# Gate tiles of a hybrid MLA and retention layer in pairs by seven block products, values of retention formed inside attention

## The chip, the cores and the metric

The kernel runs on one core of one Trainium2 chip. The metric is the device time of one execution in microseconds (us). PE is TensorE, DVE is VectorE, ACT is ScalarE, POOL is GpSimd, and SP is the engine whose queue starts nearly all transfers.

## What is computed

One decoder layer over 1024 tokens of 1024 channels, with two branches that run beside each other: MLA (8 heads) and chunkwise retention (4 heads of 256 query and key channels and 512 value channels, 8 chunks of 128 tokens). Both branches are gated and merged by sigmoid gates:

```python
mod = jax.nn.silu(c) @ w_ada[l] + b_ada[l]
shift, scale, gate = jnp.split(mod[:, None, :], 3, axis=-1)
h = rmsnorm(x, g_pre[l]) * (1.0 + scale) + shift
proj = h @ w_in[l]
(c_q, c_kv, k_pe, gate_mla, q_ret, k_ret, v_ret, gate_ret,
 merge_mla, merge_ret) = jnp.split(proj, pts, axis=-1)
y_mla = mla_branch(c_q, c_kv, k_pe, positions, g_q[l], w_q_up[l], g_kv[l], w_kv_up[l])
y_mla = y_mla * jax.nn.silu(gate_mla)
y_ret = retention_branch(q_ret, k_ret, v_ret, positions, g_ret[l]) * jax.nn.silu(gate_ret)
merged = (jax.nn.sigmoid(merge_mla) * (y_mla @ w_proj_mla[l])
          + jax.nn.sigmoid(merge_ret) * (y_ret @ w_proj_ret[l]))
x = x + gate * (merged @ w_out[l])
return rmsnorm(x, g_final)
```

The first product, `h @ w_in`, has 9,920 output columns. 5,120 of them are gates: `gate_mla` (1,024), `gate_ret` (2,048), `merge_mla` and `merge_ret` (1,024 each). `v_ret` has 2,048.

## The kernel before

**Products.** Every float32 product is made of three matmuls. Each operand is split in a high part (a copy rounded to the type that TensorE multiplies) and a low part (the operand minus its high part); high by high, low by high and high by low are summed in PSUM. A weight tile is 128 output columns by 1024 input channels, 512 KB. SP loads it into `w_raw` (`load_weight`, L428), ACT writes `w_hi` (`split_weight`, L437), DVE writes `w_lo` (`lower_weight`, L445). These three buffers have three slots (RING). A tile of `h @ w_in` is 48 matmuls of 128x512 (2 halves of the tokens, 8 blocks of input channels, 3 products) into two PSUM banks.

**Order of the weight tiles.** A list written out by hand, SEQ, gives the order in which SP, ACT, DVE and PE go through the weight tiles: first `l` (6 tiles: latents of q, of k and v, and k_pe), then `m` (8 MLA gate tiles), then one by one tiles of the up-projections (`q`, `a` and `b` with the rotary part of q, `k`, `v`; 18 to 36 or so short matmuls) and the 16 tiles `g` of retention's gate, then the 16 tiles `x` of retention's q and k, which are called turned here, with the four `v` tiles between the first of them. Gate tiles are activated by ACT and stored to DRAM (`act_t`).

**Turned tiles.** Two `x` tiles make one pair of rotated tiles: DVE multiplies each by cosine and sine (`rot_products`, L1164), POOL adds and subtracts (L837, L839), ACT and DVE split (L981, L1141) into three slots of `split_stage`, and SP stores the parts to DRAM (`store_turned`, L597; L592 stores `rot` as well for a k pair). SP does this in iteration r of one loop, which goes: load the weight tile r+4, do the loads of `w_ada_gate` for the gate row (L530, at tiles behind the last `v`), then store tile r. A load waits until the slot's old tile was lowered; SP holds everything behind an instruction that waits.

**Values of retention.** `r`: 16 weight parts, each two blocks of input channels by 512 columns, four parts for each head. Their 768 matmuls stand in a stretch of their own behind the turned tiles, one PSUM bank for each of 8 token tiles (V_BANKS), evicted in four slots of `v_stage`.

**Attention** goes in 64 steps (8 heads, 8 blocks of queries). Between its parts PE does other products as filler (`fill`, L1696), so many a step (FILL_STEP): the 16 merge gate tiles `f`, 768 matmuls. **Retention** then goes in 32 steps, and behind it the merge of both branches and the output product.

## Time and profile before

| | |
|---|---|
| three runs | 1700.97, 1701.58, 1703.8 us (median 1701.58) |
| the profiled execution | 1702.75 us, its span 1700.8 us |
| PE busy | 1653.4 us, 97% of the span |
| DVE, ACT, POOL busy | 807.4, 526.5, 76.9 us (47%, 31%, 5%) |
| DMA | 308.04 MB, 181 GB/s in the mean |

Stages by the clock of the profile, in us from the span's start: norm and modulation to about 74; `l` tiles to 109; `m` tiles to 199; up-projections and gates to 504; `v` and turned tiles to 643; values of retention to 825; attention to about 1188; then retention, merge and output. A row of the profile's timeline gives the start, the duration, the engine, the line, the operation and its tiles; in brackets stands how long the engine was idle before, and what released it.

### The profile page before, as it was taken

How to read it: one execution, taken by the hardware profiler on the slowest of the kernel's cores; microseconds unless marked ns; L12 is line 12 of the kernel's file. 1: busy time of each engine (PE TensorE's matmuls, PEld its weight loads, DVE VectorE, ACT ScalarE, POOL GpSimd, SP SyncE). 2: the span in 40 equal slices, each digit the busy share in tenths (PEclk: the TensorE clock that was granted, in tenths of full speed). 3: DMA queues.
4: the chain of work that ended last, by engine and by line, in shares of the span. 5: the costliest groups of instructions: out<-in, count | busy, mean ns of one | idle time of the engine just before them, and what ended most of it. 6: DMA issues, size and time to landing. Idle time of an engine off the chain costs nothing.

```text
span 1700.8 us, 20129 instructions
## 1 busy us (share of the span) xinstructions
PE 1653.4 (97%) x8020; PEld 1383.2 (81%) x8020; DVE 807.4 (47%) x1259; ACT 526.5 (31%) x887; POOL 76.9 (5%) x37
## 2 busy tenths in 40 slices
PE   4999999999999999999999999999899999999998
PEld 3787888888888888788788888888688887888886
DVE  6913523132345764222445555545466666545443
ACT  5443322222123211222333343434343344212211
POOL 2200001010111221000000000000000000000000
PEclk8999999999999999999999999999899999999999
DMA  9032344435377669543344444446988886523322
GB/s 388 17 109 81 107 151 149 150 130 210 130 253 256 209 209 298 209 149 146 151 158 163 154 159 163 167 140 218 382 258 275 268 268 219 209 99 136 130 89 85
DMA packets 167435, 308.04 MB, mean 181 GB/s; under 512 B 11312, under 2 KB 104368, under 8 KB 162224
## 3 DMA queue, kind: packets, MB, share of 16 engines
q1 hardware_dynamic: 167056, 306.70, 52.5%
q8 instruction: 64, 1.05, 0.2%
q14 instruction: 27, 0.22, 0.0%
q10 hardware_dynamic: 288, 0.07, 0.0%
HBM read 195.57 MB, written 110.62 MB: 180 GB/s over the span
## 4 chain that ended last, share of the span: by engine, by line
PE 88%; DVE 4%; DMA 3%; issue 2%; ACT 1%; SPq 1%; POOL 1%; ACTq 0%; DVEq 0%; POOLq 0%
PE p_banks L1696 10%; PE p_banks L1588 10%; PE p_banks L1587 10%; PE p_banks L1586 10%; PE p_banks L1726 5%; PE p_banks L1896 3%; PE p_banks L1898 3%; PE p_banks L1897 3%; PE p_banks L1645 3%; PE p_banks L1646 3%; PE p_banks L1647 3%; PE p_banks L1795 2%; PE p_banks L1946 2%; PE p_banks L1944 2%; PE p_banks L1945 2%
## 5 line engine op out<-in xcount | busy, mean ns | idle before, releaser
L445 DVE TENSOR_TENSOR w_lo<-w_raw,w_hi 128x1024 fp32r<-128x1024 f32 (+3 forms) x126 | 149.9, 1190 | 314.1 <-ACT w_hi L437 314.0
L1586 PE MATMUL p_banks<-h_hi,w_hi 128*128 128x512 f32 x688 | 269.2, 391 | 1.6 <-DVE w_lo L445 1.6
L1587 PE MATMUL p_banks<-h_lo,w_hi 128*128 128x512 f32 x688 | 267.7, 389 | 0.0
L1588 PE MATMUL p_banks<-h_hi,w_lo 128*128 128x512 f32 x688 | 267.7, 389 | 0.0
L437 ACT ACTIVATE w_hi<-w_raw 128x1024 fp32r<-128x1024 f32 x125 | 118.8, 952 | 325.7 <-PE p_banks L1647 102.2
L1586 PEld LDWEIGHTS p_banks<-h_hi,w_hi 128*128 128x128 f32 x688 | 129.2, 188 | 29.4 <-DVE w_lo L445 2.0
L1587 PEld LDWEIGHTS p_banks<-h_lo,w_hi 128*128 128x128 f32 x688 | 129.2, 188 | 27.4 <-issue 0.7
L1588 PEld LDWEIGHTS p_banks<-h_hi,w_lo 128*128 128x128 f32 x688 | 129.2, 188 | 26.7
L1696 PE MATMUL p_banks<-h_hi,w_hi 128*128 128x512 f32 x256 | 105.6, 413 | 1.8 <-DVE v_stage L1306 1.8
L1696 PE MATMUL p_banks<-h_lo,w_hi 128*128 128x512 f32 x256 | 105.3, 411 | 0.0
L1696 PE MATMUL p_banks<-h_hi,w_lo 128*128 128x512 f32 x256 | 105.1, 411 | 0.0
L1645 PE MATMUL p_banks<-w_hi,h_hi 128*128 128x512 f32 x256 | 100.9, 394 | 2.5 <-DVE v_stage L1306 2.3
L1646 PE MATMUL p_banks<-w_hi,h_lo 128*128 128x512 f32 x256 | 100.3, 392 | 0.0
L1647 PE MATMUL p_banks<-w_lo,h_hi 128*128 128x512 f32 x256 | 100.2, 391 | 0.0
L1896 PE MATMUL p_banks<-y_hi,w_hi 128*128 128x512 f32 x256 | 99.6, 389 | 0.0
L1897 PE MATMUL p_banks<-y_lo,w_hi 128*128 128x512 f32 x256 | 99.6, 389 | 0.0
L1898 PE MATMUL p_banks<-y_hi,w_lo 128*128 128x512 f32 x256 | 99.6, 389 | 0.0
L1001 ACT ACTIVATE prob<-p_banks,neg_max 128x128 f32<-128x128 f32 (+3 forms) x64 | 47.5, 742 | 143.1 <-DVE neg_max L1323 143.1
L1323 DVE TENSOR_REDUCE neg_max<-p_banks 128x1 f32<-128x128 f32 (+3 forms) x64 | 48.5, 758 | 80.1 <-PE p_banks L1758 80.1
L962 ACT ACTIVATE stage<-p_banks 128x512 f32<-128x512 f32 x48 | 26.1, 595 | 177.6 <-PE p_banks L1588 177.6
L1362 DVE TENSOR_TENSOR pt_lo<-p_banks,pt_hi 128x512 fp32r<-128x512 f32 (+2 forms) x96 | 51.8, 554 | 47.5 <-ACT pt_hi L1018 47.4
L1018 ACT ACTIVATE pt_hi<-p_banks 128x512 fp32r<-128x512 f32 (+2 forms) x96 | 46.0, 490 | 61.2 <-PE p_banks L1795 60.4
(221 smaller groups left out, 3250.2 us busy)
## 6 DMA issues: line engine op xcount, KB each, us to landing
w_raw<-in_w_dense SPq DMA_DIRECT2D x102, 512.0 KB, 5.7
act_t<-stage SPq DMA_DIRECT2D x80, 256.0 KB, 2.1
qk_chunk<-qk_chunks SPq DMA_DIRECT2D x32, 640.0 KB, 5.1
qk_chunks<-split_stage SPq DMA_DIRECT2D x32, 512.0 KB, 5.8
v_ret<-v_stage SPq DMA_DIRECT2D x32, 512.0 KB, 3.6
v_chunk<-v_ret SPq DMA_DIRECT2D x32, 512.0 KB, 5.8
merge_t<-act_t SPq DMA_DIRECT2D x48, 256.0 KB, 3.2
ada<-in_w_ada SPq DMA_DIRECT2D x4, 2048.0 KB, 23.8
```

The costliest lines, as they stand in the source:

```text
L437: self.nc.scalar.activation(self.w_hi[:, r % RING, 0:width], self.w_raw[:, r % RING, 0:width], ACT.Copy)\
L445: self.nc.vector.tensor_tensor(self.w_lo[:, r % RING, 0:width], self.w_raw[:, r % RING, 0:width], self.w_hi[:, r % RING, 0:width].bitcast( ...
L1586: nc.tensor.matmul(out, w_hi[:, slot, cut], x_hi[:, k, tok], start=(k == ks[0]), stop=False)
L1587: nc.tensor.matmul(out, w_hi[:, slot, cut], x_lo[:, k, tok], start=False, stop=False)
L1588: ins = nc.tensor.matmul(out, w_lo[:, slot, cut], x_hi[:, k, tok], start=False, stop=(k == ks[-1]))
L1645: nc.tensor.matmul(out, h_hi[:, k, tok], w_hi[:, slot, cut], start=(k == 0), stop=False)
L1646: nc.tensor.matmul(out, h_lo[:, k, tok], w_hi[:, slot, cut], start=False, stop=False)
L1647: last = nc.tensor.matmul(out, h_hi[:, k, tok], w_lo[:, slot, cut], start=False, stop=(k == KD - 1))
L1696: ins = nc.tensor.matmul(out, w[:, slot, k * P:(k + 1) * P], x[:, k, tok], start=(m == 0), stop=(m == UNIT - 1))
L1896: self.nc.tensor.matmul(out, self.w_hi[:, slot, cut], self.y_hi[y][:, tok], start=(k == 0), stop=False)
L1897: self.nc.tensor.matmul(out, self.w_hi[:, slot, cut], self.y_lo[y][:, tok], start=False, stop=False)
L1898: return self.nc.tensor.matmul(out, self.w_lo[:, slot, cut], self.y_hi[y][:, tok], start=False, stop=(k == KD - 1))
```

## The change

**Gates in pairs.** The 40 gate tiles (8 `m`, 16 `g`, 16 `f`) become 20 pairs of tiles. A pair is a product of two blocks of columns, by two halves of the input channels, by two halves of the tokens: eight block products of 12 matmuls. The change makes it by seven (`pair_products`; the seven forms of Strassen's kind): 84 matmuls of 128x512 in place of 96. For this h gets four sums over its blocks (`h_sum`, 128x2048 each, each split in two parts), and each pair four sums of weight blocks of 128x512 on POOL; ACT writes a high part for each of the seven forms (`high_form`), one copy of a product and four activations; DVE writes seven low parts and five sums of outputs (`pair_outputs`), all 128x512. A pair's weights come as one load of 1 MB (`w_pairs`). Five slots hold the forms.

**Order.** k_pe's tile comes first, then the five other latents, then all 20 pairs, then `x0` to `x5`, and then the up-projections with little between them. The norms of the latents (squares, row sums, roots, reciprocals, `c_hi`, `c_lo`) now stand beside `x0` to `x2`. SP loads tile r+3 in iteration r, where it loaded r+4. The tables of rotation and k_rope go through DRAM.

**Values of retention inside attention.** Their 768 matmuls are now the filler: FILL_START is 36 products ahead of the first scores, then FILL_STEP. The weight parts all go through slot 0 of `w_raw`, and each load waits until the part before was lowered. `v_stage` has two slots; `lower_fill` makes the low part on DVE.

The diff, cut to its core:

```diff
-SEQ = [("l", n) for n in range(LAT_TILES)] + [("m", n) for n in range(H_MLA)]
-for n in range(GATES):
-    SEQ += [UPS[n], ("g", n)]
-for n in range(TURNS):
-    SEQ += UPS[GATES + n:GATES + n + 1] + [("x", n)]
-R_UP = LAT_TILES + H_MLA
+SEQ = [("l", K_PE)] + [("l", n) for n in range(K_PE)]
+R_UP = len(SEQ)
+SEQ += [("x", n) for n in range(6)]
+SEQ += [("q", 0), ("q", 1), ("q", 2), ("q", 3), ("a", 0), ("b", 0), ("x", 6), ("q", 4), ("q", 5), ("x", 7),
+        ("q", 6), ("q", 7), ("a", 1), ("b", 1), ("x", 8), ("k", 0), ("k", 1), ("k", 2), ("k", 3), ("x", 9)]
+for n in range(4):
+    SEQ += [("k", 4 + n), ("v", n)]
+SEQ += [("x", n) for n in range(10, TURNS)]
...
+FILL_START = 36
+FILL_STEP = [12, 12, 12, 11, 11, 10, 9, 9]
...
+    def raw_place(self, r):
+
+        return self.w_raw[:, 0 if R_V <= r < R_MERGE else r % RING, 0:self.weight(r)[1]]
...
+        if R_V <= r <= R_MERGE + 1:
+            sp.wait_ge(self.w_lo_ready, r if r <= R_MERGE else R_MERGE)
...
+            self.load_weight(sp, r + RING)
...
+        self.load_weight(sp, R_V + RING)
+        sp.wait_ge(self.rot_made, self.rot_total)
+        self.load_v(sp, 0)
+        sp.wait_ge(self.gate_step, KD + 2)
...
+            nc.gpsimd.tensor_tensor(total, a21, a22, ALU.add).then_inc(self.form_sums, 1)
+            nc.gpsimd.tensor_tensor(a21, a11, a21, ALU.subtract).then_inc(self.form_sums, 1)
...
+            pe.wait_ge(self.form_lo, SUMS + f + 1)
...
+            for q in range(KD // 2):
+                cut = slice(q * P, (q + 1) * P)
+                self.nc.tensor.matmul(out, w_hi[:, cut], x_hi[:, q, :], start=fresh and q == 0, stop=False,
+                                      skip_group_check=True)
+                self.nc.tensor.matmul(out, w_hi[:, cut], x_lo[:, q, :], start=False, stop=False, skip_group_check=True)
+                last = self.nc.tensor.matmul(out, w_lo[:, cut], x_hi[:, q, :], start=False, stop=q == KD // 2 - 1,
+                                             skip_group_check=True)
...
+        self.fill(pe, FILL_START)
...
+            if tile == 0 and not first and kind == 0:
                 pe.wait_ge(self.w_lo_ready, r + 1)
```

SP's queue at the end of the turned tiles, before: L428 loads a weight, L530 a block of `w_ada_gate`, L592 and L597 store a k pair, L597 alone a q pair; the last rows are k pair `x15`, the gate row, and the first loads for attention.

```order
L428 DMA w_raw<-in_w_dense 128x1024 [waits w_lo_ready] x2
L592 DMA qk_chunks<-rot 128x8x128 [waits rot_added]
L597 DMA qk_chunks<-split_stage 128x8x128 [waits split_lo_ready]
L597 DMA qk_chunks<-split_stage 128x8x128
L592 DMA qk_chunks<-rot 128x8x128 [waits rot_added]
L597 DMA qk_chunks<-split_stage 128x8x128 [waits split_lo_ready]
L597 DMA qk_chunks<-split_stage 128x8x128
L428 DMA w_raw<-in_w_dense 128x1024 [waits w_lo_ready]
L552 DMA gate_rows<-gate_row 128x1024 [waits gate_step]
L428 DMA w_raw<-in_w_dense 128x1024 [waits w_lo_ready] x2
L604 DMA q_even<-q_hl 128x2048 [waits split_stored_2,split_stored_1,rot_stored,split_stored_0,gate_row_stored]
```

The same place after the change, from behind the stores of `x11` on; here L469 loads a weight, L640 a block of `w_ada_gate`, L702 stores. The first L469 loads `x15`, the next four the first four value parts.

```order
L469 DMA w_raw<-in_w_dense 128x1024 [waits w_lo_ready]
L640 DMA ada_gate_w<-in_w_ada_gate 128x1024 [waits gate_step] x2
L469 DMA w_raw<-in_w_dense 128x1024 [waits w_lo_ready]
L640 DMA ada_gate_w<-in_w_ada_gate 128x1024 [waits gate_step] x2
L702 DMA qk_chunks<-split_stage 128x8x128 [waits split_lo_ready]
L702 DMA qk_chunks<-split_stage 128x8x128
L702 DMA qk_chunks<-split_stage 128x8x128 [waits split_lo_ready]
L702 DMA qk_chunks<-split_stage 128x8x128
L469 DMA w_raw<-in_w_dense 128x1024 [waits w_lo_ready]
L646 DMA k_rope<-k_rope 128x2048 [waits split_stored_2,ret_tables_stored,split_stored_1,split_stored_0]
```

Behind these rows come the loads for the first head, the load of the third part, the six stores of `x15`, and the load of the fourth part. The loads of the value parts moved in between gate row blocks and stores, and four of them are wanted at once.

PE at the start of attention after the change: L1845 is the row sum for the gate row, L1927 the filler, L1985 the first scores; each wait for `w_lo_ready` is for one value part.

```order
L1845 MATMUL p_banks<-gate_row,ones 128x512 [waits split_lo_ready,gate_step]
L1845 MATMUL p_banks<-gate_row,ones 128x512
L1927 MATMUL p_banks<-w_hi_aside,h_hi 128x512 [waits rot_products,w_lo_ready]
...
L1927 MATMUL p_banks<-w_hi,h_hi 128x512 [waits w_lo_ready]
...
L1927 MATMUL p_banks<-w_hi,h_hi 128x512 [waits w_lo_ready]
...
L1927 MATMUL p_banks<-w_hi,h_hi 128x512 [waits w_lo_ready]
...
L1985 MATMUL p_banks<-k_even,q_even 128x128 [waits late_consts_loaded,consts_split,ret_tables_loaded,gate_step,qk_even_loaded]
```

Six filler products stand between one wait for a part and the next, and the row sum now stands at the very end of the turned tiles, where it stood three tiles behind the last gate block.

## Rows read from the trace of the kernel before

**Rows 1.** The page: busy time and share of the span, by engine.

```profile
PE 1653.4 (97%) x8020; PEld 1383.2 (81%) x8020; DVE 807.4 (47%) x1259; ACT 526.5 (31%) x887; POOL 76.9 (5%) x37
```

**Rows 2.** Windows: stretch, its length, busy time of PE, PEld, DVE, ACT, POOL, PE clock, DMA.

```profile
109.00:199.00 90.00, 90.00 (x391) 73.15 (x390) 42.00 (x27) 35.68 (x42) 0.00 (x0) 1.00 0.24 81
504.00:643.00 139.00, 137.93 (x670) 115.97 (x669) 88.41 (x70) 32.88 (x39) 28.22 (x10) 1.00 0.71 232
643.00:825.00 182.00, 179.53 (x782) 146.49 (x781) 46.93 (x50) 38.51 (x47) 4.76 (x2) 0.99 0.53 186
825.00:1188.00 363.00, 361.02 (x2081) 313.83 (x2081) 185.75 (x378) 143.82 (x310) 0.00 (x0) 1.00 0.48 167
```

**Rows 3.** Timeline of PE: two matmuls, 66 apart in a gapless stretch.

```profile
184.30 0.39 PE L1586 MATMUL p_banks<-h_hi,w_hi 128*128 128x512 f32 x1
...
199.26 0.39 PE L1586 MATMUL p_banks<-c_hi,w_hi 128*128 128x512 f32 x1
```

**Rows 4.** Waits of PE over the span: total, times, longest.

```profile
PE p_banks L1811 <- DMA qk_chunk<-qk_chunks: 7.2, 2, 6.4
...
PE p_banks L1645 <- DVE v_stage L1306: 2.3, 4, 1.6
```

**Rows 5.** Timeline of PE at the start of attention.

```profile
827.24 0.47 PE L1696 MATMUL p_banks<-h_hi,w_hi 128*128 128x512 f32 x1 [1.81 <-DVE v_stage L1306]
...
829.20 0.63 PE L1696 MATMUL p_banks<-h_hi,w_lo 128*128 128x512 f32 x1
829.63 0.63 PE L1696 MATMUL p_banks<-h_hi,w_hi 128*128 128x512 f32 x1
```

**Rows 6.** Timeline behind a second turned tile (k pair): DVE.

```profile
556.34 2.35 DVE L1164 TENSOR_TENSOR rot<-p_banks,ret_tables_back 128x1024 f32<-128x1024 f32 x2 [1.69 <-PE p_banks L1588]
558.61 2.51 DVE L445 TENSOR_TENSOR w_lo<-w_raw,w_hi 128x1024 fp32r<-128x1024 f32 x1
561.16 4.58 DVE L1141 TENSOR_TENSOR split_stage<-rot,split_stage 128x1024 fp32r<-128x1024 f32 x2
...
574.09 1.22 DVE L445 TENSOR_TENSOR w_lo<-w_raw,w_hi 128x1024 fp32r<-128x1024 f32 x1
```

**Rows 7.** The same pair: POOL, SP's queue; then a q pair: DVE, SP.

```profile
557.64 2.39 POOL L837 TENSOR_TENSOR rot<-rot 128x1024 f32<-128x1024 f32 x1 [28.62 <-DVE rot L1164]
...
570.57 1.70 SPq L428 DMA_DIRECT2D w_raw<-in_w_dense  x1
...
522.49 1.23 DVE L1164 TENSOR_TENSOR rot<-p_banks,ret_tables_back 128x1024 f32<-128x1024 f32 x1 [2.21 <-PE p_banks L1588]
...
534.10 1.81 SPq L428 DMA_DIRECT2D w_raw<-in_w_dense  x1
```

**Rows 8.** A k pair beside the gate row's blocks: DVE, SP's queue, DVE, ACT.

```profile
599.85 2.36 DVE L1164 TENSOR_TENSOR rot<-p_banks,ret_tables_back 128x1024 f32<-128x1024 f32 x2 [3.77 <-PE p_banks L1588]
...
622.11 2.57 SPq L428 DMA_DIRECT2D w_raw<-in_w_dense  x2
...
626.74 2.67 DVE L1296 SCALAR_TENSOR_TENSOR gate_row<-ada_gate_w,silu_c,gate_row 128x1024 f32<-128x1024 f32 x2
...
629.61 1.06 ACT L437 ACTIVATE w_hi<-w_raw 128x1024 fp32r<-128x1024 f32 x1 [17.75 <-DMA w_raw<-in_w_dense]
```

**Rows 9.** DMA issues, KB and us to landing: windows 130:430 (two), 601:645.

```profile
w_raw<-in_w_dense SPq DMA_DIRECT2D x20, 512.0 KB, 5.7
w_raw<-in_w_q_up SPq DMA_DIRECT2D x12, 192.0 KB, 3.0
...
w_raw<-in_w_dense SPq DMA_DIRECT2D x4, 512.0 KB, 7.3
```

**Rows 10.** Groups of DVE's instructions, window 100:504: busy, mean ns, idle before.

```profile
L1273 DVE RECIPROCAL latent_total<-latent_total 128x1024 f32<-128x1024 f32 x2 | 13.1, 6554 | 3.4 <-ACT latent_total L918 3.4
...
L1280 DVE TENSOR_TENSOR latent<-latent,latent_total 128x1024 f32<-128x1024 f32 x5 | 5.8, 1219 | 0.0
```

**Rows 11.** Timeline of ACT at the first `v` tile.

```profile
506.53 0.60 ACT L981 ACTIVATE split_stage<-p_banks 128x512 fp32r<-128x512 f32 x1 [5.28 <-DMA qk_chunks<-split_stage]
```

More of the change, by code:

```diff
@@ L34 @@
 ACT_TILES = 40
-MASKED = -1e30
+MASKED = -2.0 ** 100
 TURN_1 = 6.28125
@@ L374, in counts @@
             elif kind in "abx":
+                self.rot_pair[r], self.k_turns[r] = rot // 4, turned
+                turned += kind == "x" and i % 4 == 3
                 rot += 2
@@ L521, in sync @@
                 sp.dma_start(self.ret_tables[:, :, :], d["ret_tables"].rearrange("a p n -> p a n"))\
                     .then_inc(self.tables_loaded, 16)
+            for n, out in enumerate((1, 0, 2, 3)):
+                tile, half = ((0, 0), (1, 1), (1, 0), (0, 1))[out]
+                sp.wait_ge(self.evicted, self.latent_evicted + 5 * pair + 2 + n)
+                sp.dma_start(d["act_t"][2 * pair + tile][:, half * HALF:(half + 1) * HALF], self.out_stage[out])\
+                    .then_inc(self.stored[out], 16)
@@ L523, in sync @@
+        for r in range(R_UP, R_V):
+            kind, i = SEQ[r]
+            self.load_weight(sp, r + RING)
             if r == R_GATE_ROW:
@@ L713, in sync_retention @@
                 self.load_t(sp, 1)
-            if n == 4:
-                for half in range(2):
-                    sp.wait_ge(self.stored[half], 16 * (H_MLA + GATES + FILL_TILES))
             if n + 3 < CHUNK_STEPS:
@@ L1241, in vector @@
+        self.lower_weight(dve, R_UP + 2)
+        for n, (b, i, squares) in enumerate(((0, 1, 3), (0, 2, 4), (1, 4, 5))):
+            dve.wait_ge(self.squared, NT + squares)
+            if n == 1:
+                dve.wait_ge(self.lat_added, 1)
+            nc.vector.tensor_tensor(self.total[:, b, :], self.total[:, b, :], self.places[i], ALU.add)\
+                .then_inc(self.lat_added, 1)
+        for r in range(R_UP, R_V):
+            kind, i = SEQ[r]
             if kind in "qk":
@@ L1655, in tensor, with pair_products @@
         self.tensor_output(pe)
+    def pair_products(self, pe, pair):
+        h = [self.h_hi, self.h_lo]
+        even, odd = (slice(e, KD, 2) for e in range(2))
+        low, high = slice(0, HALF), slice(HALF, S)
+        sums = [(self.h_sum_hi[n], self.h_sum_lo[n]) for n in range(SUMS)]
+        operands = [[x[:, even, low] for x in h], sums[0], sums[1], sums[2], [x[:, odd, low] for x in h], sums[3],
+                    [x[:, odd, high] for x in h]]
+        for n in range(FORMS):
+            f = FORMS * pair + n
+            out = self.p[:, self.form_bank(pair, (0, 1, 2, 3, 0, 4, 1)[n]), :]
+            fresh = n not in (4, 6)
+            pe.wait_ge(self.form_lo, SUMS + f + 1)
+            if n == 0:
+                if pair < 2:
+                    pe.wait_ge(self.evicted, self.latent_evicted - 2)
+                else:
+                    pe.wait_ge(self.pair_done, SUMS + 5 * (pair - 1))
+            elif pair == 0 and n in (1, 2):
+                pe.wait_ge(self.evicted, self.latent_evicted - 2 + n)
+            elif pair and n == 3:
+                pe.wait_ge(self.evicted, self.latent_evicted + 5 * pair - 2)
+            elif n == 4:
+                pe.wait_ge(self.evicted, self.latent_evicted + 5 * pair + 1)
+            elif pair and n == 5:
+                pe.wait_ge(self.pair_done, SUMS + 5 * pair)
+            elif n == 6:
+                pe.wait_ge(self.pair_done, SUMS + 5 * pair + 3)
+            w_hi, w_lo = (self.form[f % FORM_SLOTS][:, low_part, :] for low_part in range(2))
+            x_hi, x_lo = operands[n]
+            for q in range(KD // 2):
[5 more added lines that the diff above has]
+                                             skip_group_check=True)
+            last.then_inc(self.form_summed, 1)
     def v_up(self, pe, r):
```

828 lines of the change are left out of this document (479 added, 349 removed).

## The prediction

> **What bounds the kernel now.** I read the page first: PE is busy 97% of the span, DVE 47%, ACT 31%, POOL 5% [rows 1], so PE's stream sets the time, and an engine beside it matters where it keeps PE waiting. Then the windows, to see where PE is idle: 0 in the 90 us of gates, 1.1 us in the turned tiles (139.00 − 137.93), 2.5 in the values of retention, 2.0 in attention [rows 2]. Then the pace: two matmuls 66 apart start 14.96 us apart, so one of 128x512 costs 0.2267 us, whatever the 0.39 of its record [rows 3]. At that pace the 768 matmuls of the values are 174.1 us, and their stretch ran from 643.3 to 824.7: some 7.2 us more than its work. The waits of PE name v_stage for 2.3 of them, and the chunks of retention for 7.2 us elsewhere [rows 4]. Attention starts with a wait of 1.81 us [rows 5].
>
> The clock shows there too: behind that wait matmuls start 0.43 us apart in place of 0.23 (829.20, 829.63) [rows 5], which is the lower of the two levels (1.2 and 2.4 GHz), for about 10 matmuls, 2 us. So the start of attention costs 3.8 us.
>
> **What is removed.** 40 gate tiles of 48 matmuls become 20 pairs of 84: 1,920 − 1,680 = 240 matmuls, 240 × 0.2267 = **54.4 us** [rows 3]. The stretch of the values goes: its 768 matmuls take the place of the 768 of the merge gates in attention, at the same price, and its 7.2 us of stalls with it; so do the 3.8 at the start of attention and the 1.1 of the turned tiles. Gains: 54.4 + 7.2 + 3.8 + 1.1 = **66.5 us**.
>
> **What is added beside PE.** A pair gives PE 84 × 0.2267 = 19.0 us. DVE gets 12 instructions of 128x512 in it; one of 128x1024 takes 1.22 us [rows 10], half of it 0.61, with a fixed part some 0.69: 8.3 us. ACT gets 12 of about 0.6: 7.1. POOL gets 4 sums; one of 128x1024 takes 2.39 [rows 7], half of it 1.2: 4.8. All lie under 19.0, and the forms are made up to four ahead, so I cost them at nothing. If POOL and DVE slow each other, the trace has a price: the w_lo of 558.61 took 2.51 us, POOL working from 557.64 on, and that of 574.09 took 1.22 [rows 6, 7]. All seven low parts at double price would make DVE 13 us a pair, still under 19.0.
>
> The Trainium skill speaks against this placing of sums: its page "SBUF — State Buffer", under "SBUF: two separate sides", says that a DVE instruction with both inputs in SBUF and a GpSimd one that reads SBUF exclude each other for the whole instruction. By that rule the two engines' times add up, 8.3 + 4.8 = 13 us, and the pair stays bound by PE; the trace agrees with the rule (2.51 beside 1.22).
>
> The four sums of h and their splits go on DVE ahead of the first pair, beside the latents' tiles; an estimate from instructions of 1.22 us for 1,024 columns has the first low part ready at 109 us, when PE ends the latents; bounds 0 and 3 us, I take 1.
>
> **What moves, projections.** Before, each short up-projection tile had a full tile of 10.9 us behind it. Now they stand in a row, and SP loads tile r+3 right behind the stores of tile r−1. Behind a k pair's second tile that load goes out 14.2 us after PE ends (556.34 to 570.57), behind a q pair's 11.6 (522.49 to 534.10) [rows 6, 7]. It lands in 3.0 us for a q tile, 5.7 for a full one, 7.3 under stores [rows 9], and then come w_hi and w_lo (1.1 us for a short tile, 2.3 to 3.6 for a full one [rows 6, 8]). So the fourth tile behind a turned pair can't start before +17 to +19 us, and the three in between cover it for 48 × 0.2267 = 10.9 each if full, but 18 × 0.2267 = 4.1 if `q`, 2.7 if `k`.
>
> - DVE first: x0 to x2 (32.6 us of PE) carry the two reciprocals 13.1, five products 5.8, c_lo about 6.2, squares' sums 3.7 [rows 10], beside two or three rotations 2.35, low parts 1.2 to 2.5 and splits 4.6 [rows 6]: 46 in all, begun at 10.9, the end of x0. So DVE is at 57 then, at 62 with x3's rotation and a w_lo; x3's splits are out at 70 and q1's weight is lowered at 76.3, where PE is there at 6 × 10.9 + 4.1 = 69.4: q1 waits 6.9.
> - x5, then q0, q1, q2 (12.3 us): q3 waits 7.3, with DVE's lateness in it.
> - x7, then q6, q7, a1: 14.2 + 0.5 + 3.0 + 1.1 = 18.8, less 12.3: 6.5; I take 6.3 (4.8 to 7.8).
> - k0 to k2 (8.2) cover the load of x9 (5.7 and 2.3, and the store ahead): 3.9.
> - x9, then k4, v0, k5 (11.1): v1 waits 5.9. The splits of v0 to v3 wait for stores to leave the three slots, as before, where one such wait was 5.28 us and full tiles hid it [rows 11]: 1.8 for v1, 4.2 for v2, 4.3 for v3. Small ones 0.9.
>
> Sum 6.9 + 7.3 + 6.3 + 3.9 + 7.7 + 4.2 + 4.3 + 0.9 = 41.5, call it **42 us**. Nothing excludes that waits merge, since a stall gives SP time for the next: low end 15; high end 50.
>
> **What moves, into attention.** I count from the end of x11, where PE has 43.6 us of x12 to x15 left. SP issues the stores of x11 and then the load of x15 at +22.3 (599.85 to 622.11) [rows 8]; it lands at 29.8 (7.3 [rows 9]) and is lowered at 32. Blocks 2 and 3 of the gate row are added at 34.6 (2.67 for two [rows 8]). The first value part is loaded at 35.7, lowered at 43.7. Then x13's splits, 46; blocks 4 and 5, 48.6; its four stores and the loads of blocks 6 and 7 to 53; the second part lands at 60.5, is lowered at 62.7; blocks 6 and 7 are added at 65.3. Only then can the row sum run, for which PE has waited since 43.6: 21.7 us. The third part is lowered at about 72. The fourth waits in SP behind the six stores of x15: issued at 78, lowered at 87.9. PE wants it after the row sum and 18 products, nominally at 49.4. So PE loses 87.9 − 49.4 = **38 us** up to the first scores; what lies behind DVE and SP there (scores, softmax) has nothing else to run on. Low end 8 if the loads are not held by the gate row, high end 45.
>
> In attention the parts come one by one through one slot; 16 − 4 loads over 64 steps of 5.7 us (363 / 64 [rows 2]) leave the time, but at the three changes of head the lowering must fit behind the last use: 0 to 6, I take **2**. At the start of retention three more loads of 512 KB join the chunks, which PE already waits 7.2 us for [rows 4]: 0 to 5, I take **2**. The clock falls after each long wait; at 2 us each [rows 5] and some eight waits, half of them where PE waits anyway: 5 to 16, I take **7**.
>
> The Trainium skill, page "TensorE: Matmul & The Clock Gate", under "HAM oscillation — how this bites in real kernels", says that waits for DMA throttle PE again and again, and cost beyond the wait itself. The trace agrees (0.43 for 0.23 us), and this is a point against the change that a count of matmuls misses.
>
> **Sum**, against the profiled execution's 1702.75 (span 1700.8, 1.2 above the median of the runs): 1702.75 − 66.5 + 42 + 38 + 2 + 2 + 1 + 7 = 1728.3; less 1.2: **1727 us** as a median.
>
> **The rivals.**
> (B) It gets faster: one mechanism, that PE's waits in the projections let SP run ahead, so the loads around the gate row go out early and the transition costs the 8 us of its low end, while the projections keep 30. 1702.75 − 66.5 + 30 + 8 + 12 − 1.2 = 1685. For it: SP's lateness is counted from PE's ends, and each stall gives it time. Against: at 622.11 the load was late though no tile before it was [rows 8]. It turns faster when both terms together fall under 54 us.
> (C) Weight tiles hide everywhere, as before the waits of PE in these stages were few [rows 2]: 1701.6 − 66.5 + 7 = 1642.
> (D) The seven products are bound by POOL or DVE after all, if a sum of 128x512 on POOL costs 3 us and more, as a fixed part would make it: 2 us a pair, 40 on top: 1767.
> (E) No change, gains and waits equal: 1698 to 1705.
>
> **How the numbers follow.** A measurement of this kernel tells about 0.2%, 3.4 us, from no change. My forecast (own range 1712 to 1745) has 0.67, B 0.13, C 0.07, D 0.08, E 0.05. Slower is forecast and D, 0.75; same 0.05; faster B and C, 0.20. The range leaves C and D out (0.15) and a little at B's edge: 1679 to 1750.
>
> **What would show it.** In the profile after: 240 matmuls fewer on PE; the pairs with PE gapless for 380 us (20 × 19.0); waits of PE for w_lo before q1, q3, b1, x9, v1; and for the gate row and w_lo at L1845 and L1927, some 38 us in a place. SP's queue should show the fourth value part's load behind the stores of x15. I am wrong if PE is not idle at L1845 and L1927, or if the forms wait for POOL.

## The result and the profile after

The changed kernel takes 1791.06 us in the median of four runs (1788.92 to 1795.02), the kernel before 1701.28: a ratio of 1.0527 with a 95% interval of 1.0506 to 1.0548. It is slower by 90 us, where 25 were forecast, and outside the range of 1679 to 1750. The page of the profile after, busy time by engine and the clock granted to PE in 40 slices of the span:

```profile
PE 1625.2 (91%) x7780; PEld 1353.8 (76%) x7780; DVE 940.2 (53%) x1467; ACT 579.9 (32%) x1005; POOL 188.0 (11%) x117
...
PEclk8999999999998989997899999989899999999999
```

PE has the 240 matmuls less (7,780 for 8,020 [rows 1]), and is busy 28.2 us less in a span that is 86.2 us longer (1787.0 for 1700.8). So its idle time grew from 47.4 to 161.8 us, by 114.4. 240 matmuls are 54.4 us; busy time fell by 26.2 less than that. Most of these 26.2 are matmuls at the lower clock: by the clock's records PE is busy for 67.1 us at the lower level, where it was 21.4, and half of the difference is 22.8; the other 3.4 are not assigned. Below, "the clock" stands for the whole 26.2. 114.4 + 26.2 − 54.4 = 86.2: that is the whole result, and it falls into stages. Windows (length, busy time of PE, PEld, DVE, ACT, POOL, clock, DMA):

```profile
109.00:490.00 381.00, 380.34 (x1677) 314.65 (x1678) 174.69 (x242) 141.79 (x242) 108.15 (x78) 1.00 0.30 111
490.00:760.00 270.00, 228.81 (x1033) 188.38 (x1032) 148.04 (x124) 73.74 (x93) 35.89 (x14) 0.92 0.55 188
760.00:870.00 110.00, 72.07 (x290) 56.92 (x289) 45.76 (x37) 16.16 (x16) 15.15 (x6) 0.83 0.69 222
870.00:1252.00 382.00, 353.88 (x1985) 305.25 (x1984) 192.97 (x390) 135.13 (x296) 0.00 (x0) 0.96 0.46 161
1262.00:1310.00 48.00, 28.45 (x141) 23.33 (x140) 20.98 (x53) 14.88 (x29) 0.00 (x0) 0.79 0.93 342
```

The first is the pairs: PE gapless at full clock, 20 pairs in 381 us. The seven products do what they are for. The others are the projections, the last turned tiles with the start of attention, attention, and the start of retention. PE's waits give the same places by what ended them (us in total, times, longest):

```profile
PE p_banks L1796 <- DVE w_lo L495: 31.5, 6, 8.2
PE p_banks L1845 <- DVE gate_row L1472: 20.2, 1, 20.2
PE p_banks L1958 <- DVE w_lo L495: 19.6, 1, 19.6
PE p_banks L1985 <- ACT prob L1156: 18.2, 3, 6.7
PE p_banks L1927 <- DVE w_lo L495: 17.7, 2, 14.7
...
PE p_banks L2007 <- DMA v_head<-v_hl: 9.9, 3, 3.5
PE p_banks L1903 <- DVE w_lo L495: 8.0, 2, 7.4
...
PE p_banks L1903 <- DVE split_stage L1304: 3.3, 3, 1.5
...
PE p_banks L1885 <- DVE w_form L1423: 1.1, 1, 1.1
```

L1796 and L1903 are the projections: 31.5 + 8.0 + 3.3 = 42.8 us. L1845 and L1927 are the gate row and the value parts at the start of attention: 37.9. L1985 and L2007 are attention: 28.1. L1985 makes the scores, which wait until ACT has made the exp of the step before (`prob`); L2007 makes the products with v. L1958 is the merge product that fills retention: 19.6, where the wait of 7.2 for chunks is gone [rows 4].

How these waits come about is read from the queues. In the projections, the longest one (8.18 us, before q1) reads like this, with DVE, SP and ACT (SPq is SP's queue):

```profile
550.57 2.35 DVE L1324 TENSOR_TENSOR rot<-p_banks,ret_tables_back 128x1024 f32<-128x1024 f32 x2
...
560.52 3.32 SPq L702 DMA_DIRECT2D qk_chunks<-split_stage  x2
563.88 3.10 SPq L469 DMA_DIRECT2D w_raw<-in_w_q_up  x2
...
570.92 1.00 ACT L489 ACTIVATE w_hi<-w_raw 128x384 fp32r<-128x384 f32 x2 [12.87 <-DMA w_raw<-in_w_q_up]
```

SP issues q1's weight right behind the last stores of x2 and x3, and ACT stands 12.87 us until it lands. The stores are late because DVE came to the rotation of x3 only at 550.57, 12.7 us after PE had ended x3 (537.9), behind the low parts of the latents. So both causes of the prediction are in this one wait: DVE is late, and the place of the load behind the stores hands that on.

In attention, SP and ACT and PE around 950 us:

```profile
949.88 0.32 SPq L771 DMA_DIRECT2D v_ret<-v_stage  x1
950.24 0.43 SPq L469 DMA_DIRECT2D w_raw<-in_w_dense  x1
...
954.43 1.06 ACT L489 ACTIVATE w_hi<-w_raw 128x1024 fp32r<-128x1024 f32 x1 [8.46 <-DMA w_raw<-in_w_dense]
955.40 0.99 ACT L1156 ACTIVATE prob<-p_banks,neg_max 128x896 f32<-128x896 f32 x1
...
956.53 0.80 PE L1985 MATMUL p_banks<-k_odd,q_odd 128*128 128x512 f32 x1 [5.99 <-ACT prob L1156]
```

The value part's load is issued behind a value store, for whose low part SP waits; ACT stands 8.46 us for the load, and the exp of the step stands behind it on ACT. PE's wait is put down to the exp, which is ready in a microsecond. The load of v_head has the same neighbour:

```profile
923.34 0.32 SPq L771 DMA_DIRECT2D v_ret<-v_stage  x1
923.70 0.58 SPq L719 DMA_DIRECT2D v_head<-v_hl  x1
```

At the start of retention, the chain of what ended last:

```profile
1273.93 2.82 SPq L798
1276.86 4.69 SPq L851
...
1283.23 10.11 DMA v_ret<-v_stage
...
1294.01 1.05 ACT w_hi L489
```

and ACT's timeline there:

```profile
1293.43 0.69 ACT L1183 ACTIVATE v_stage<-p_banks,ret_cols 128x512 fp32r<-128x512 f32 x1 [20.11 <-DMA v_ret<-v_stage]
```

ACT stands 20.1 us before the eviction of the last value unit, since the unit before it has the same stage slot and its store was issued late and took 10 us; the high part of the merge weight that PE wants stands behind it.

And nearly every long wait leaves the clock low, as in [rows 5]. PE waits 15 times over 2 us behind the pairs; after 13 of these waits the clock's records have the lower level for another 3 to 6 us. Here behind the one of 8.18 us:

```profile
572.09 0.79 PE L1796 MATMUL p_banks<-c_hi,w_hi 128*128 128x512 f32 x1 [8.18 <-DVE w_lo L495]
...
573.53 0.63 PE L1796 MATMUL p_banks<-c_hi,w_hi 128*128 128x512 f32 x1
573.96 0.63 PE L1797 MATMUL p_banks<-c_lo,w_hi 128*128 128x512 f32 x1
```

### The profile page after: what moved, and what is told of

Read it like the earlier page. It is cut to its first block, busy times and chain, and to the rows that moved or that the text cites. A ratio compares the mean times of both kernels' runs of the same rounds, so it can differ in the third digit from the quotient of the medians.

```text
span 1787.0 us, 20246 instructions
## 1 busy us (share of the span) xinstructions
PE 1625.2 (91%) x7780; PEld 1353.8 (76%) x7780; DVE 940.2 (53%) x1467; ACT 579.9 (32%) x1005; POOL 188.0 (11%) x117
## 4 chain that ended last, share of the span: by engine, by line
PE 71%; DVE 9%; DMA 9%; SPq 3%; POOL 2%; issue 2%; ACT 2%; ACTq 0%; DVEq 0%; POOLq 0%
PE p_banks L1927 9%; PE p_banks L1885 7%; PE p_banks L1887 7%; PE p_banks L1888 7%; DMA w_raw<-in_w_dense 5%; PE p_banks L1958 5%; PE p_banks L2132 3%; PE p_banks L2131 3%; PE p_banks L2130 3%; PE p_banks L2029 2%; SPq L702 2%; PE p_banks L2180 2%; PE p_banks L2179 2%; PE p_banks L2178 2%; DVE split_stage L1304 1%
## 5 line engine op out<-in xcount | busy, mean ns | idle before, releaser
L489 ACT ACTIVATE w_hi<-w_raw 128x1024 fp32r<-128x1024 f32 (+3 forms) x81 | 72.3, 894 | 371.0 <-DMA w_raw<-in_w_dense 157.6
L495 DVE TENSOR_TENSOR w_lo<-w_raw,w_hi 128x1024 fp32r<-128x1024 f32 (+2 forms) x82 | 94.8, 1157 | 143.1 <-ACT w_hi L489 143.0
L1423 DVE TENSOR_TENSOR w_form<-w_pair,w_form 128x512 fp32r<-128x512 f32 x120 | 92.9, 775 | 102.0 <-ACT w_form L1090 100.8
L1090 ACT ACTIVATE w_form<-w_pair 128x512 fp32r<-128x512 f32 x120 | 75.6, 632 | 195.1 <-PE p_banks L1888 187.1
L1796 PE MATMUL p_banks<-h_hi,w_hi 128*128 128x512 f32 x304 | 120.8, 397 | 7.6 <-DVE w_lo L495 7.6
L1797 PE MATMUL p_banks<-h_lo,w_hi 128*128 128x512 f32 x304 | 119.4, 393 | 0.0
L1798 PE MATMUL p_banks<-h_hi,w_lo 128*128 128x512 f32 x304 | 119.3, 392 | 0.0
L1927 PE MATMUL p_banks<-w_hi,h_hi 128*128 128x512 f32 x192 | 80.7, 420 | 17.7 <-DVE w_lo L495 17.7
L1885 PE MATMUL p_banks<-h_hi,w_form 128*128 128x512 f32 x240 | 93.5, 389 | 1.1 <-DVE w_form L1423 1.1
L1888 PE MATMUL p_banks<-h_hi,w_form 128*128 128x512 f32 x240 | 93.4, 389 | 0.0
L1887 PE MATMUL p_banks<-h_lo,w_form 128*128 128x512 f32 x240 | 93.4, 389 | 0.0
L1927 PE MATMUL p_banks<-w_lo,h_hi 128*128 128x512 f32 x192 | 80.6, 420 | 0.0
L1927 PE MATMUL p_banks<-w_hi,h_lo 128*128 128x512 f32 x192 | 80.2, 418 | 0.0
L1796 PEld LDWEIGHTS p_banks<-h_hi,w_hi 128*128 128x128 f32 x304 | 57.7, 190 | 21.3 <-DVE w_lo L495 8.9
L1958 PE MATMUL p_banks<-y_hi,w_hi 128*128 128x512 f32 x128 | 52.1, 407 | 19.6 <-DVE w_lo L495 19.6
```

The source lines that it names most:

```text
L495: self.nc.vector.tensor_tensor(self.lo_place(r), self.raw_place(r), self.hi_place(r).bitcast(F32), ALU.subtract)\
L1796: nc.tensor.matmul(out, w_hi[:, slot, cut], x_hi[:, k, tok], start=(k == ks[0]), stop=False)
L1797: nc.tensor.matmul(out, w_hi[:, slot, cut], x_lo[:, k, tok], start=False, stop=False)
L1798: ins = nc.tensor.matmul(out, w_lo[:, slot, cut], x_hi[:, k, tok], start=False, stop=(k == ks[-1]))
L1885: self.nc.tensor.matmul(out, w_hi[:, cut], x_hi[:, q, :], start=fresh and q == 0, stop=False, skip_group_check=True)
L1887: self.nc.tensor.matmul(out, w_hi[:, cut], x_lo[:, q, :], start=False, stop=False, skip_group_check=True)
```

## The experiments

All are the changed kernel with edits; times are medians, beside 1791.06 for the changed kernel and 1701.3 to 1702.2 for the kernel before, which was measured again beside each. Waits and busy times are those of the one profiled execution of each run. Where an edit adds or removes lines, the line numbers of its run differ a little.

**A slot of its own for the last value unit** (retention's start).

```diff
-        return 0 if unit == FILL_UNITS - 1 else unit % 2
+        return 2 if unit == FILL_UNITS - 1 else unit % 2
```

> The changed kernel, but the last of the 32 value units gets a stage slot of its own. Theory: the 19.6 us for which PE waits at the start of retention (L1958 for w_lo) are a queue's: ACT stands for 20.1 us in the eviction of the last unit, since the unit before it has the same slot and its store is late, and the high part of the first merge weight stands behind it on ACT. Then the wait falls to 4 to 10 us, and the time by 10 to 16, to about 1778. Rival: the three weights themselves land late there, among the chunks of retention at 342 GB/s. Then the wait stays at 15 to 20 and the time within 4 us of 1791.

1785.0 us, 6 less. The wait at L1958 fell from 19.6 to 5.9, as the theory had it, but a new one of 4.6 us for a chunk of q and k came, and PE's busy time rose by 6.1. The cause of the 19.6 is shown; removing it gives less than its size.

**Value stores one step later.**

```diff
-            while units < self.units_filled(g):
+            while units < self.units_filled(g - 1):
                 self.store_fill(sp, units)
```

> The changed kernel, but SP stores a value unit one step later in attention, so that its wait for the unit's low part no longer stands ahead of that step's loads. Theory: the value stores hold SP, and behind them the load of v_head (PE waits 9.9 us in three places) and the next value part (ACT waits for w_raw with the exp behind it, PE 18.2 us in three places). Then v_head's waits fall under 2 us, those for exp to 8 or less, and the time by 15 to 25, to about 1771. Rival: both are late because they take long to land (6.8 and 4 to 10 us), or because the one slot makes each load wait for the lowering of the part before: then the waits stay within 4 us of 28 and so does the time of 1791.

1761.6 us, 29 less, a little more than the theory's most. v_head's waits are gone (9.9 to 0.3), those for exp fell from 18.2 to 11.9, and PE's busy time by 9.6, the clock that comes back with them. So the place of one wait in SP's queue was worth 29 us. What is left of the waits for exp is nearly one wait, 11.50 us at 1153.87: ACT stands there 15.05 us for a value part that was issued behind the v, q and k loads of a head. The run with the loads apart, below, takes that up.

**Another order of tiles**, with x5 to x9 between the q tiles.

```diff
+SEQ += [("x", n) for n in range(5)]
+SEQ += [("q", 0), ("x", 5), ("q", 1), ("q", 2), ("x", 6), ("q", 3), ("x", 7), ("q", 4), ("q", 5), ("x", 8),
+        ("q", 6), ("x", 9), ("q", 7), ("a", 0), ("b", 0), ("a", 1), ("b", 1), ("k", 0), ("k", 1), ("k", 2), ("k", 3)]
```

> The changed kernel with another order of the tiles behind the pairs: x5 to x9 stand between the q tiles, one full tile for one or two short ones, so that three tiles behind each turned pair are 19 us or more except once; the work is the same. Theory: the 42.8 us that PE waits there (31.5 + 8.0 + 3.3) come from loads that are issued behind the stores of turned tiles, three tiles ahead, and the short tiles don't cover them. Then they fall to 10 to 22 us, the time with the clock by 25 to 35, to about 1761. Rival: DVE is the one that is late, from the latents' reciprocals and products on. Then q0 and q1 wait as long or longer, the sum stays above 33, and the time falls by less than 10.

1788.9 us, 2 less: the theory's numbers failed, and the rival's came out (above 33 us of waits, less than 10 us of time). The waits in the projections went from 42.8 to 36.5 (32.4 + 1.7 + 2.4). PE's timeline shows where the long ones are now:

```profile
571.88 0.80 PE L1796 MATMUL p_banks<-c_hi,w_hi 128*128 128x512 f32 x1 [6.07 <-DVE w_lo L495]
...
667.86 0.80 PE L1796 MATMUL p_banks<-c_hi,w_hi 128*128 128x512 f32 x1 [6.03 <-DVE w_lo L495]
...
686.53 0.79 PE L1796 MATMUL p_banks<-c_hi,w_hi 128*128 128x512 f32 x1 [5.46 <-DVE w_lo L495]
...
701.62 0.79 PE L1796 MATMUL p_banks<-c_hi,w_hi 128*128 128x512 f32 x1 [6.47 <-DVE w_lo L495]
```

Three of the four lie at 667 to 702 us, where this order has x9, q7, a0, b0, a1, b1 and the k tiles in a row. The first of the three is a load behind the stores of x9, with the short q7, a0 and b0 for cover. The other two stand behind the stores of b0 and b1 (`qr_hl` in SP's queue at 678.30 and 693.69): I had counted the x pairs and forgotten that `b` tiles are rotated, split and stored as well. The fourth, q1's, fell only from 8.18 to 6.07, as its load kept its place: behind the stores of x3, issued at 563.69, where it was 563.88. So the order moved waits and gained nothing, and it does not decide between the two theories. The next run but one does: with the load ahead of the stores q1 waits 1.42 us, though DVE comes to the rotation of x3 hardly earlier (547.99 for 550.57).

**Six of the gate row's eight blocks left out.**

```diff
-            if 0 <= r - R_GATE_ROW < KD // 2:
+            if 0 <= r - R_GATE_ROW < 1:
```

> The changed kernel without six of the eight blocks of the gate row (their loads on SP and their instructions on DVE); the gate row holds the first two blocks only. Theory, one chain: the four value parts go through one slot and SP's stores, and the gate row is only in between; its row sum no longer waits, but PE then waits for the parts, and of the 37.9 us lost there 27 to 33 stay: time down by 5 to 11, to about 1783. Rival: the gate row's blocks are what bounds the place (20.2 us at the row sum). Then 20 us or more go, to 1770 or less.

1779.8 us, 11 less. The wait at the row sum went (20.2 to 0), and that for the parts rose from 17.7 to 23.9. Of 37.9 us 23.9 stayed, less than the 27 to 33 of the theory but more than the 17.9 or less that the rival leaves: the gate row and the parts are one chain, of which the row is a little over a third.

**The load of tile r+4 in iteration r**, as before the change.

```diff
+        self.load_weight(sp, R_UP + RING)
         for r in range(R_UP, R_V):
             kind, i = SEQ[r]
-            self.load_weight(sp, r + RING)
+            self.load_weight(sp, r + RING + 1)
```

> The changed kernel, but SP loads weight tile r+4 in iteration r behind the pairs, as before the change, so the load goes out ahead of the stores of tile r where it stood behind them. Theory: the waits in the projections come from the load's place behind a turned pair's stores; with one tile more of cover (4.1 us for a q tile, 2.7 for a k tile, 10.9 for a full one) each falls by that: 42.8 us to 15 to 25, and the value parts go out earlier too, so of the 37.9 us at the start of attention 25 to 32 stay. Time down by 25 to 40, to about 1758. Rival: the three slots and the stores' waits bound it, not the place of the load: less than 10 us.

1762.0 us, 29 less. The waits in the projections fell from 42.8 to 26.0, those at the start of attention from 37.9 to 15.6 (its waits of PE: L1845 2.9, L1927 12.7), which is just short of the forecast for the first (15 to 25) and far below it for the second (25 to 32). And 8 us came back as waits for exp:

```profile
PE p_banks L1985 <- ACT prob L1156: 26.5, 5, 7.8
...
PE p_banks L1796 <- DVE w_lo L495: 14.6, 5, 6.3
PE p_banks L1927 <- DVE w_lo L495: 12.7, 2, 10.0
PE p_banks L1903 <- DVE split_stage L1304: 11.4, 4, 6.8
```

So one place of the load in a loop made half of the loss of both stages together (80.7 us to 41.6). The new wait for exp is one of 7.77 us at 848.82, where ACT stands 12.12 us for a value store.

**The fourth value part's load ahead of the stores of x15.**

```diff
             self.load_weight(sp, r + RING)
+            if r == R_V - 1:
+                self.load_weight(sp, R_V + RING)
```

> The changed kernel, but SP loads the fourth value part ahead of the six stores of x15. Theory: the 14.7 us that PE waits for it at L1927 are in part SP's, which issues the load at 854.6 where the part before was lowered at about 847.5: 5 to 8 us less, time to about 1784. Rival: the load shares the DMA engines with the stores and the loads for the first head, and lands as late: within 3 us of 1791.

1794.0 us, no gain. Its waits of PE:

```profile
PE p_banks L1986 <- ACT prob L1157: 27.9, 5, 8.5
...
PE p_banks L1928 <- DVE w_lo L495: 6.9, 2, 4.8
```

The part did come earlier (17.7 to 6.9, 10.8 less, more than the theory said), and 9.7 us came back at once as waits for exp in attention (18.2 to 27.9). The rival's number came out, but not its reason. Nearly all of the new wait is one place, 8.47 us at 883.83, and ACT shows what it is:

```profile
882.42 0.69 ACT L1184 ACTIVATE v_stage<-p_banks,ret_cols 128x512 fp32r<-128x512 f32 x1 [12.83 <-DMA v_ret<-v_stage]
```

ACT stands for a value store, which SP issued at 870.55 behind the loads for the next heads, and the exp stands behind that eviction. It is the same place as in the run before: when PE comes earlier to attention, it meets the next limit, which the wait for the part had covered. Neither theory had that. The run with the first two value stores ahead of these loads, below, removes the same wait from the three edits.

**The weight sums on DVE in place of POOL.**

```diff
+                nc.vector.tensor_tensor(total, a21, a22, ALU.add).then_inc(self.form_sums, 1)
+                nc.vector.tensor_tensor(a21, a11, a21, ALU.subtract).then_inc(self.form_sums, 1)
...
+                nc.vector.tensor_tensor(a11, total, a11, ALU.subtract).then_inc(self.form_sums, 1)
...
+                nc.vector.tensor_tensor(a12, a12, a11, ALU.subtract).then_inc(self.form_sums, 1)
```

> The changed kernel, but DVE makes the four weight sums of each pair, and POOL none. Theory: the pairs are bound by PE with slack on every other engine; DVE gets some 2.8 us a pair to its 9 and gives back what POOL slows in it (a low part of 128x512 takes 0.775 us on average, 0.69 without POOL). The pairs stay at 380 us and the time within 4 us of 1791. Rival: the forms are just in time; then 20 pairs lose 1 to 3 us each, 20 to 60 us.

1790.5 us, no difference. The window of the pairs, here in this run, has PE gapless with either:

```profile
130.00:490.00 360.00, 360.00 (x1590) 298.07 (x1589) 197.58 (x297) 131.46 (x225) 0.00 (x0) 1.00 0.31 113
```

DVE has 198 us of work in 360, where it had 163 with the sums on POOL, and there is room for more. The forecast's term of nothing for the work beside PE is shown.

**Last slot, later stores and lead of four together.**

> The changed kernel with the edits of the last slot, the later value stores and the lead of four together. Theory: the three hold in different places, so they add: 6 + 29 + what the lead of four gives alone (25 to 40), time 1716 to 1731, still slower than the kernel before. Rival: they share one cause, the queue of SP, and overlap by more than 15 us.

1722.3 us, 69 less than the changed kernel. Alone they gave 6.1, 29.5 and 29.1, 64.7 in sum: three places that add, as the theory had it. In the profiled executions PE's idle time falls by 61.0 us, where the three alone give 60.9 in sum; the 4 us between 69 and 65 are within the spread of the run with the lead of four (1755.59 to 1765.37). What is left in attention reads like this; SP's queue and ACT:

```profile
1107.60 0.46 SPq L469 DMA_DIRECT2D w_raw<-in_w_dense  x1
...
1120.47 1.06 ACT L489 ACTIVATE w_hi<-w_raw 128x1024 fp32r<-128x1024 f32 x1 [13.27 <-DMA w_raw<-in_w_dense]
```

The weight was issued in time and landed 12.9 us later, behind the loads of v, q and k of a head that went out at 1101.6 to 1106.6 (3.5 MB) and two value stores (1 MB).

**Value parts split behind the exp**, on ACT and DVE at the end of a step.

```diff
-            while parts < self.parts_used(g - 2):
-                self.split_weight(act, R_V + V_PARTS + parts)
-                parts += 1
...
+            while parts < self.parts_used(g - 2):
+                self.split_weight(act, R_V + V_PARTS + parts)
+                parts += 1
             if g == STEPS + 1:
                 self.high_chunk(act, 0)
```

> The three edits together (last slot, later value stores, lead of four), and in attention the high and the low part of a value weight stand at the end of a step on ACT and DVE, where they stood ahead of the exp. Theory: PE's waits for exp there, 18.0 us in three places with the three edits, are ACT's queue: it stood 13.3 us for a weight that landed 12.9 us after it was issued, behind the q, k and v loads of a head, with the exp behind it. Then they fall to 8 or less and the time by 8 to 14 from 1722, to about 1711. Rival: the products want the part as early, and the wait moves to L1927 for w_lo: time within 4 us of 1722.

1726.8 us, 4.5 more than without it, and no execution of either run reaches the other's range. The waits for exp are 17.2 (from 18.0) and v_head's are back at 4.2. The theory falls, and the rival's L1927 is not it either (14.1 from 12.6): at 1130.51 ACT still stands 9.58 us for the value part, now at the end of a step, and the exp of the next step comes behind it (PE waits 7.97 there, for 10.22). The other wait, 9.23 at 852.26, had another cause, which the next run but one removes.

**The same with the spread order**, so with the value parts behind the exp too.

> The same with the order of the tiles in which x5 to x9 stand between the q tiles. Theory: 24 us of waits are left in the projections with a lead of four tiles, behind turned pairs whose cover is four short tiles; spread they fall by 8 to 15, the time to about 1700, near the kernel before. Rival: as with a lead of three tiles, where the same order gave 2 us, the waits only move to other tiles: within 4 us of the run without it.

1725.7 us, 1 less, within the spread. 22.2 us of waits are left in the projections (15.5 + 6.7) for 26.2: they are many short ones now. The rival holds. The runs that follow leave both of these edits out and start from the three edits again.

**The first two value stores ahead of the next heads' loads.**

```diff
+        for unit in range(2):
+            self.store_fill(sp, unit)
         self.load_qk(sp, 1)
```

> The three edits together (last slot, later value stores, lead of four), and at the start of attention SP issues the first two value stores ahead of the q, k and gate loads for the next heads (3.3 MB), where they stood behind. Theory: with the three edits PE waits 7.2 us for exp at 851.5, since ACT stands 11.6 us before it for a value store that was issued behind those loads, and the exp stands behind that eviction. Then this wait goes, the waits for exp fall from 18.0 to about 11 and the time from 1722 to about 1714. Rival: the transfers share the engines whatever the order, and the store or the head's loads are late as before: within 4 us of 1722.

1712.3 us, 10 less than the three edits. The waits for exp fell from 18.0 to 12.0. ACT had stood 11.6 us for a store that was issued behind 3.5 MB of loads: two gate tiles (1.0), and q and k of the second head (2.5), which starts eight steps later. The one long wait for exp that is left is 11.27 us at 1111.12.

**Loads apart**: q and k of a head two steps behind its v, those of the first head one tile earlier.

```diff
-                if h + 1 < H_MLA:
-                    self.load_qk(sp, h + 1)
+            if i == 4 and 1 <= h < H_MLA - 1:
+                self.load_qk(sp, h + 1)
...
-            if r == R_GATE_ROW + 4:
+            if r == R_GATE_ROW + 3:
```

> The same, and the loads of a head's q and k go out two steps behind its v in place of right behind it, and those of the first head one tile earlier. Theory: the wait of 10.2 us for exp at 1122 is a value weight that landed 12.9 us after its issue behind 3.3 MB of one head's loads; with only v ahead of it the weight lands some 6 us earlier, and the four parts at the start of attention some 3 us earlier. Waits for exp under 6 us, the time 6 to 12 under the run without it, about 1704: near the kernel before, by 66 us of gains less the 26 us in the projections, about 14 at the start of attention, 9 in retention and the clock. Rival: the loads collide with the stores of y and of values two steps on: within 4 us of the run without it.

1709.0 us, 3 less. The waits for exp halved again (12.0 to 6.0), those for the value parts rose from 12.4 to 17.1. Two edits at once, so the next run takes the second back:

> The run with the loads apart, but the first head's q and k loads at the tile where they stood, not one earlier. Theory: those loads, one tile earlier, stood ahead of the third value part and made PE wait 4.7 us longer at L1927's place for w_lo (17.1 for 12.4); the loads of later heads two steps behind v gave the 6.0 us of exp. Then w_lo there is back at 12 to 13, exp stays under 7, and the time is 1703 to 1706. Rival: the two edits belong together, and exp's waits come back: 1709 to 1713.

1706.6 us in eleven runs (1700.86 to 1708.84), a ratio of 1.0023 (1.0014 to 1.0032) to the kernel before. Waits for exp 5.9, as said (under 7); for the parts 14.2, between the 12 to 13 of the theory and the 17.1 of the run before; the time just above the 1703 to 1706 of the theory. This is the best version, 84 us under the changed kernel and still 4.6 over the one before.

**The first head's loads behind the fourth part.**

```diff
-            if r == R_GATE_ROW + 4:
+            if r == R_V - 1:
```

> The same, but the first head's loads stand behind the load of the fourth value part, ahead of the stores of x15. Theory, transfers ahead: the third and fourth part land 4 to 6 us earlier, PE waits 7 to 9 us for them in place of 12 to 13, and some of it comes back as a wait of the first scores for q and k (0 to 4 us): time 1697 to 1703. Rival, the chain: each part waits for the lowering of the one before, whatever lies in the transfers, or the first scores wait for all that is gained: within 3 us of the run without this edit.

1712.5 us, 6 more. Its waits of PE:

```profile
PE p_banks L1987 <- ACT prob L1158: 13.1, 4, 7.3
...
PE p_banks L1929 <- DVE w_lo L495: 7.0, 2, 4.5
```

7.2 us less for the parts, 7.2 more for exp. The median is above both forecasts (1697 to 1703, and within 3 us of 1706.6). The new wait is one of 7.31 us at 834.43, for the first exp, and ACT stands for the stores of x15 (18.03 us), which SP now issues directly behind the first head's loads:

```profile
832.62 1.28 ACT L1158 ACT_TABLE_LOAD   x1 [18.03 <-DMA qk_chunks<-split_stage]
```

So at this place the third and fourth part, the first head's loads and the stores of x15 are all wanted within some 20 us, and each order that was tried made PE wait for one of them.

## Why the prediction was wrong

The direction held and the size did not: 25 us were forecast and 90 came. The step that failed is the list of places where PE waits. It priced the waits inside attention and at the start of retention at 2 us each, and they cost 28.1 and 12.4; and with them the clock, at 7 for 26.2. By its own steps, all against 1702.75 of the profiled execution:

- **The gain of matmuls, 54.4, held**: 240 fewer, at 19.0 us a pair (381 us for 20). **The work beside PE at nothing held**, also with POOL's sums on DVE. The first form came 1.1 us late; I had taken 1.
- **The projections, 42, held at 42.8**, with the five long waits at the tiles named: q1 8.18 (6.9 forecast), q3 7.74 (7.3), b1 7.92 (6.3), x9 4.79 (3.9), v1 7.41 (7.7). Together these are 36.0 for 32.1. The waits of v2 and v3, put at 4.2 and 4.3, were 1.5 and 2.3. So the sum is closer than its terms, and that part is luck. The mechanism, a load behind a turned pair's stores with short tiles for cover, is supported by the lead of four, which took 17 us of them; DVE's lateness for q1 is in the trace as well (x3's rotation at 550.57), but it costs 1.42 us once the load no longer stands behind the stores. The order with x5 to x9 spread did not remove the waits.
- **Into attention, 38, held at 37.9** (20.2 + 17.7; forecast 21.7 + 16.8), and the fourth part's load was issued behind x15's stores, as said. The times inside the chain held too, counted from the end of x11: row sum at 63.9 (65.3 forecast), second part lowered at 61.3 (62.7), fourth issued at 81 (78) and lowered at 90 (87.9). The run without the gate blocks and the lead of four support the one chain.
- **"In attention ... 0 to 6, I take 2" failed: 28.1.** I asked when a part would be wanted by PE and found time enough. I did not ask what stands behind the waiting instructions: on ACT the exp behind the split of a part, on SP the next part and v_head behind a store that waits for its low part. Moving only that store gave 29.5 us. The rest has two more neighbours of the same kind, with a large load ahead: a part behind the v, q and k loads of a head, and a value store behind the loads for the next heads. With both moved 5.9 us of waits for exp are left.
- **"At the start of retention ... I take 2" failed: 19.6, less the 7.2 that went.** I counted three loads more among the chunks. The cost was a stage slot shared by the last two units, which holds ACT until a store has landed. With a slot of its own 5.9 of the 19.6 are left and a wait of 4.6 comes beside it, 10.5 us for the 7.2 before: 3.3 more, where I had 2.
- **The clock, 7 (5 to 16), was mis-sized: 26.2.** I took eight waits at 2 us and thought half of them free. PE waits over 2 us 15 times behind the pairs, and after 13 of them it works 3 to 6 us at the lower level, which costs 1.5 to 3 us each.
- **The gains of 12.1 in stalls** were a little high: of the 114.4 us more of idle time 1.1 + 42.8 + 37.9 + 28.1 + 12.4 = 122.3 are named above, so 7.9 went. The rest of the 12.1 were slow matmuls, which are in the clock's 26.2.
- **Rival D** (the forms wait for POOL) did not come: a sum takes 1.3 to 1.7 us and not 3. Its own price does not carry it either, since four sums at 3 us are 12 us, under the 19.0 of a pair.

Together: 26.1 for attention, 10.4 for retention, 19.2 for the clock and 4.2 for the gains are 59.9 of the 60.6 us between the 1728.3 forecast for the profiled execution and its 1788.92. None of the rivals was this one: B had SP run ahead by PE's stalls, and it did not. My range ended at 1750 because its bounds came from the same list of places. The waits that I missed sit where the change put a transfer's wait into a queue that carries work for others. I followed the queues only up to the first scores.

The best version is still 4.6 us over the kernel before, and the profile says where: its span is 1703.7 and PE's busy time 1615.3, so against the kernel before it is idle 41.0 us more and busy 38.1 less. 23.0 of its waits are in the projections, 17.7 at the start of attention, 8.5 in retention, 5.9 for exp, and the lower clock takes 16.3 of the 54.4. What stays open is whether these can go. The start of attention was tried three ways and only exchanged one wait for another; that nothing better is possible there isn't shown. And no run has the pairs without the values inside attention, so what the two halves of the change are worth apart is read from the stages and not measured.

## What to carry to other kernels

A saving in the bound engine's instructions is worth what the queues leave of it: here 54.4 us of matmuls were really saved, at a cost of 1.1 us where they were saved, and 114.4 us of idle time and 26.2 of clock were paid where other work had lost its cover. When a change adds a load, a store or an eviction to a stream, list for SP and for each engine what stands behind the instruction that waits, and price the first of these that the bound engine wants, not the transfer itself. And where PE's wait is put down to an engine whose instruction is short, as the exp here, look at what that engine stood for just ahead of it. When a wait is removed, look again: another limit may have been hidden behind it, as the value store was behind the wait for the fourth part.

## What was not expected of the hardware

- A load of 512 KB, 4.4 to 7.3 us in the median of three stretches of the kernel before, took 12.9 us when it was issued 1 us behind 3.5 MB of other loads and directly behind 1 MB of stores on the same queue. In crowded stretches SP's own issue rows grow too: 4.69 us for one load at 1276.86 (L851, shown above), where 0.4 us is usual.
- The clock cost as much as a large wait: 26.2 us, for 15 waits over 2 us. With the value stores one step later PE was idle 20.0 us less, and its busy time fell by 9.6 us with that.
- POOL beside DVE cost little. The low parts of the forms, with and without POOL's sums (mean ns of one):

```profile
L1423 DVE TENSOR_TENSOR w_form<-w_pair,w_form 128x512 fp32r<-128x512 f32 x120 | 92.9, 775 | 102.0 <-ACT w_form L1090 100.8
```

```profile
L1418 DVE TENSOR_TENSOR w_form<-w_pair,w_form 128x512 fp32r<-128x512 f32 x120 | 82.9, 691 | 83.8 <-ACT w_form L1073 83.0
```

The first is the changed kernel, the second the one with the sums on DVE: 84 ns each in the mean, 10 us over 120 records. The mean hides two cases: 20 of the 120, about one a pair, take 1.0 to 1.2 us, and each of them meets a sum on POOL; the 100 others take the 0.7 us of the run without these sums. The Trainium skill, "SBUF — State Buffer", section "SBUF: two separate sides", has the two engines exclude each other for whole instructions. The trace agrees: an instruction that meets POOL is longer by some 0.5 us, and the others by nothing.
